# GDN's head norm moved into its back part, tokens on partitions

## The chip, the cores and the metric

One core of one Trainium2 chip. The metric is the device time of one execution in microseconds; the kernel before took 2085.72 us, the median of three runs (2085.12 to 2091.74).

## The reference, cut to what matters

The kernel computes three layers' worth of blocks in float32 for 528 tokens (16 meta tokens and 512) of width 1024. The change touches the first one, a gated delta net with 16 value heads of width 128, and in it the step between the recurrence and the output product:

```
o = chunk_gated_delta_rule(q, k, v, g, beta)
o = rms_norm(o, w_norm) * jax.nn.silu(z.reshape(b, t, GDN_V_HEADS, GDN_HEAD_DIM))
return o.reshape(b, t, GDN_V_DIM) @ w_out

def rms_norm(x, w):          # over the 128 features of one head and token
    return x * rsqrt(mean(x * x, axis=-1) + 1e-6) * w
```

## The kernel before, in words

The kernel is a row of stages, each a block with one program per engine; a stage ends when all engines have ended. Weights come in units of 128x2048 floats into one of four slots of `raw`; ScalarE casts a unit into a high part `whi` (`split_hi`, L153), VectorE makes the low part `wlo` (`split_lo`, L158), and every product of weights is three passes of TensorE over these (`product`).

The gated delta net has four stages. `gdn_front` makes q, k, v, z and the gates; v and z are spilled to DRAM. `gdn_back` (L1574) runs the recurrence. `head_norm` (L845) normalizes the heads, and `gated_down` (L2008) multiplies them with SiLU(z) and with the output weights.

`gdn_back` works on 20 units: 5 chunks (one of the 16 meta tokens, four of 128 tokens) by 4 groups of 4 heads. The software pipeline runs slots t = -1 to 22; `step(t, ...)` of each engine says which part of which unit it does in slot t, and in which order. That order is written out by hand, and each engine goes through it in order, with waits on semaphores. In slot t TensorE prepares unit t+1 (`prepare`: key-query products, transposed keys and values), multiplies the state for unit t (`old_values`), solves for unit t-1 (`new_values`), and makes the state's update and the output of unit t-2 (`update`, `output`). ScalarE copies the output of unit t-3 out of PSUM (`outputs`, L1829), exponentiates decays (`decays`, `weights`), copies the new values (`news`, L1824) and scales the values (`values`, L1816). VectorE multiplies by the decays (`attention` L1873, `differ` L1879), subtracts (`residual` L1890), makes the decayed copy of the new values (`decayed` L1898) and advances the state (`states` L1910). GpSimd adds the mask and multiplies q (L1658, L1664).

Slots 0 to 15 carry beside this the two last levels of the inversion of the 64 triangular matrices (`turn5` L1737 to `close6` L1764 on TensorE, `copy5`, `copy6` on ScalarE, `corner5` L1917, `corner6` on VectorE). TensorE's `open6` (L1756) waits for VectorE's `corner5`. In slots 0 to 7 VectorE also eliminates inside the 32x32 blocks of the second half (`second_half`, L1386 and L1389).

The output product (L1728, L1729) has the state and the new values as the stationary operand, so its result has features on partitions and tokens in rows: `ob`, one bank of PSUM, is the only one for it. ScalarE copies it to `qkv`, where q was (`out`). `yt` and the `raw` slots are the same memory; SP loads the first three units of the output weights there as the chunks are done with it (`ahead`).

`head_norm` goes over the 16 heads: GpSimd squares 128x528, TensorE sums over partitions with a matrix of ones, ScalarE takes Ln and Exp, VectorE multiplies by gain and root in place. The engines work on different heads at the same time.

`gated_down` splits units 0 and 1 first. Its SP program loads the fourth weight unit and then 16 tiles of z of 264 KB, three at a time. ScalarE takes their SiLU, VectorE the product with the heads, and both split it into high and low; TensorE uses each of the 16 tiles for units 0 and 1 as it comes, then runs units 2 to 7.

Of the kernel before, what the change touches and what calls it, by code (L numbers as in the profile page):

```python
# [23 lines left out]
P = 128  # L24
# [124 lines left out]
def split_hi(k, act, u, slot, used):  # L149

    act.wait_ge(k.raw_landed[slot], landed_value(u, slot))
    if used is not None:
        act.wait_ge(k.tile_full, used)  # L153
    k.nc.scalar.copy(k.whi[:, slot % SPLIT_SLOTS, :], k.raw[:, slot, :]).then_inc(k.hi_done, 1)  # L154


def split_lo(k, eng, u, slot):

    eng.wait_ge(k.hi_done, u + 1)
    s = slot % SPLIT_SLOTS  # L160
    eng.tensor_tensor(k.wlo[:, s, :], k.raw[:, slot, :], k.whi[:, s, :].bitcast(F32),  # L161
                      ALU.subtract).then_inc(k.lo_done, 1)
# [37 lines left out]
def unit_tiles(k, pe, u, slot, kts, xhi, xlo, first_slot, tile_free, x_ready=None):  # L200
# [4 lines left out]
    whi = k.whi[:, s, :].rearrange("p (k n) -> p k n", k=kts)  # L205
    wlo = k.wlo[:, s, :].rearrange("p (k n) -> p k n", k=kts)
# [559 lines left out]
def weight_ring(k, name, ctx):  # L766
    sb = lambda nm, shape, dt: ctx.enter_context(k.nc.sbuf_tensor(f"{name}_{nm}", shape, dt))
    k.whi, k.wlo = sb("whi", [P, SPLIT_SLOTS, UNIT], F32R), sb("wlo", [P, SPLIT_SLOTS, UNIT], F32R)
# [74 lines left out]


def head_norm(k, name, n, tile, ones, scale, gain, gain_src=None, then=(), gain_parts=()):  # L845

    nc = k.nc
    with ExitStack() as ctx:  # L850
        sb = lambda nm, shape: ctx.enter_context(nc.sbuf_tensor(f"{name}_{nm}", shape, F32))
        sq, rinv = sb("sq", [P, 4, T]), sb("rinv", [P, 4, T])
        g = sb("g", [P, n])
        sem = lambda nm: k.sem(f"{name}_{nm}")
        gain_in, squared, summed, log, inv, done = (sem(x) for x in (
            "gain_in", "squared", "summed", "log", "inv", "done"))
        gain_set = sem("gain_set")
        past4 = lambda j: not (isinstance(j, int) and j < 4)
        block = ctx.enter_context(stage(k))

        @block.sync
        def _(sp):
            if gain_src is not None:
                with nc.allow_non_contiguous_dma(reason="gains, feature on partitions"):
                    sp.dma_start(g[:, 0:gain_src.shape[1]], gain_src).then_inc(gain_in, 16)
            if then:
                load_ahead(k, sp, k.unit, then)

        @block.gpsimd
        def _(pool):  # L870
            def square(j, b):
                if past4(j):
                    pool.wait_ge(summed, j - 3)
                pool.tensor_tensor(sq[:, b, k.now], tile(j)[:, k.now], tile(j)[:, k.now], ALU.mult).then_inc(squared, 1)
            for cols, value in gain_parts:
                pool.memset(g[:, cols], value).then_inc(gain_set, 1)
            rounds(pool, n, square, 4)

        @block.tensor
        def _(pe):  # L880
            def one(j, b):
                pe.wait_ge(squared, j + 1)
                if past4(j):
                    pe.wait_ge(log, j - 3)
                for hf, half in enumerate(k.halves):
                    mm = pe.matmul(k.ps[b][:, hf, 0:k.width], ones, sq[:, b, half], start=True, stop=True)
                mm.then_inc(summed, 1)
            rounds(pe, n, one, 4)

        @block.scalar  # L890
        def _(act):
            def logarithm(j, b):
                act.wait_ge(summed, j + 1)
                if past4(j):
                    act.wait_ge(done, j - 3)
                nc.scalar.activation(parted(k, rinv[:, b, k.now]), filled(k, k.ps[b]), ACT.Ln, scale=scale,
                                     bias=k.eps[:, :])\
                    .then_inc(log, 1)
            def one(j, b):
                if not (isinstance(j, int) and j == n - 1):  # L900
                    logarithm(j + 1, (b + 1) % 4)
                act.wait_ge(log, j + 1)
                nc.scalar.activation(rinv[:, b, k.now], rinv[:, b, k.now], ACT.Exp, scale=-0.5).then_inc(inv, 1)
            nc.scalar.preload_act_table_set("natural_log_exp_and_others")
            logarithm(0, 0)
            rounds(act, n, one, 4)

        @block.vector
        def _(dve):
            if gain_src is not None:  # L910
                dve.wait_ge(gain_in, 16)
            if gain_parts:
                dve.wait_ge(gain_set, len(gain_parts))
            def one(j, b):
                dve.wait_ge(inv, j + 1)
                dve.scalar_tensor_tensor(out=tile(j)[:, k.now], in0=tile(j)[:, k.now], scalar=gain(g, j),
                                         in1=rinv[:, b, k.now], op0=ALU.mult, op1=ALU.mult).then_inc(done, 1)
            rounds(dve, n, one, 4)
# [655 lines left out]
def gdn_back(k, g, qkv, an, d, tmp, yt, yt0, out_unit):  # L1574
# [13 lines left out]
    with ExitStack() as ctx:  # L1588
# [32 lines left out]
        def _(sp):  # L1621
# [45 lines left out]
        def _(pe):  # L1667
# [50 lines left out]
            def output(u):  # L1718
# [11 lines left out]
                mm.then_inc(s.o_ready, 1)  # L1730
            def turn5(u):
# [35 lines left out]
            def step(t, real, level):  # L1767
# [22 lines left out]
        def _(act):  # L1790
            out = qkv[:, 0:2 * GQ, :].rearrange("p (o q) t -> p o q t", o=2)
# [33 lines left out]
            def outputs(u):  # L1825
                c, i = units[u]
                n, t = size(c), first_token(c)
                act.wait_ge(s.o_ready, u + 1)
                nc.scalar.copy(out[:, :, 2 * i:2 * i + 2, t:t + n],  # L1829
                               ob[:, :, 0:n].rearrange("p (q o) n -> p o q n", o=2)).then_inc(s.o_done, 1)  # L1830
# [12 lines left out]
            def step(t, real, level):  # L1843
# [1916 lines left out]
```

## Time and profile before

| what | value |
|---|---|
| median of three runs | 2085.72 us |
| the profiled execution: its time, its span | 2096.65 us, 2094.9 us |
| granted TensorE clock, mean | 0.951 |
| busy: TensorE, VectorE, ScalarE, GpSimd | 93%, 52%, 41%, 9% |
| back part of GDN, first and last instruction | 354 to 567.5 us |
| head norm | 567.8 to 593.4 us |
| output stage, first cast and first product | 593.7, 603.5 us |

The profile comes from one execution, slower than the median; differences are made within it. Granted clock 1.00 is 2.4 GHz and 0.50 is 1.2 GHz. "Idle before" names who released an engine that stood still. The slots of the back part can be told by ScalarE's copy of an output (L1829) at the start of each from t = 3 on:

| slot t | L1829 starts at, us |
|---|---|
| 3, 4, 5 | 389.47, 405.31, 420.80 |
| 6, 7, 8, 9 | 432.09, 443.29, 454.51, 464.65 |
| 10 to 15 | 474.05, 483.43, 492.82, 502.20, 511.58, 520.97 |
| 16 to 19 | 530.35, 537.36, 543.96, 550.55 |
| 20, 21, 22 | 557.72, 562.01, 566.30 |

### The profile page before, as it was taken

How to read it: one execution, taken by the hardware profiler on the slowest of the kernel's cores; microseconds unless marked ns; L12 is line 12 of the kernel's file. 1: busy time of each engine (PE TensorE's matmuls, PEld its weight loads, DVE VectorE, ACT ScalarE, POOL GpSimd, SP SyncE). 2: the span in 40 equal slices, each digit the busy share in tenths (PEclk: the TensorE clock that was granted, in tenths of full speed). 3: DMA queues.
4: the chain of work that ended last, by engine and by line, in shares of the span. 5: the costliest groups of instructions: out<-in, count | busy, mean ns of one | idle time of the engine just before them, and what ended most of it. 6: DMA issues, size and time to landing. Idle time of an engine off the chain costs nothing. (4 is left out here: it accounts for less than half of the span.)

```text
span 2094.9 us, 31713 instructions
## 1 busy us (share of the span) xinstructions
PE 1953.2 (93%) x12868; PEld 1744.9 (83%) x12868; DVE 1087.9 (52%) x1779; ACT 851.6 (41%) x1364; POOL 181.4 (9%) x198
## 2 busy tenths in 40 slices
PE   7999998999869999999999987899999998899988
PEld 6999998889769999999999965678888885787666
DVE  6657667675583344343453366544444447852243
ACT  6557742345472332333333144443332333424342
POOL 0001221022320000000000031000000002000101
PEclk9999998589989999999999999999999999999999
DMA  7223451113254223222222222223223322311101
GB/s 179 88 72 122 120 161 47 31 47 75 68 142 103 77 85 96 86 92 88 90 73 81 84 59 64 81 80 101 89 93 100 99 82 62 121 54 48 41 1 40
DMA packets 205246, 173.91 MB, mean 83 GB/s; under 512 B 41232, under 2 KB 180496, under 8 KB 205128
## 3 DMA queue, kind: packets, MB, share of 16 engines
q1 hardware_dynamic: 205128, 172.25, 27.7%
q8 instruction: 84, 1.38, 0.3%
q14 instruction: 34, 0.28, 0.0%
HBM read 161.40 MB, written 10.83 MB: 82 GB/s over the span
## 5 line engine op out<-in xcount | busy, mean ns | idle before, releaser
L161 DVE TENSOR_TENSOR main_wlo<-raw,main_whi 128x2048 fp32r<-128x2048 f32 x106 | 242.8, 2291 | 312.0 <-ACT main_whi L154 312.0
L154 ACT CAST main_whi<-raw 128x2048 fp32r<-128x2048 f32 x106 | 201.6, 1904 | 475.4 <-PE ps L176 474.1
L176 PE MATMUL ps<-ffn_xhi,main_whi 128*128 128x264 f32 (+1 forms) x768 | 206.5, 323 | 6.6 <-DVE ffn_xlo L646 6.6
L176 PE MATMUL ps<-ffn_xhi,main_wlo 128*128 128x264 f32 (+1 forms) x768 | 206.7, 324 | 0.0
L176 PE MATMUL ps<-ffn_xlo,main_whi 128*128 128x264 f32 (+1 forms) x768 | 206.6, 323 | 0.0
L176 PE MATMUL ps<-ffn_ahi,main_wlo 128*128 128x264 f32 (+1 forms) x768 | 205.2, 322 | 0.0
L176 PE MATMUL ps<-ffn_alo,main_whi 128*128 128x264 f32 (+1 forms) x768 | 205.0, 321 | 0.0
L176 PE MATMUL ps<-ffn_ahi,main_whi 128*128 128x264 f32 (+1 forms) x768 | 203.8, 320 | 0.0
L176 PE MATMUL ps<-gdn_xhi,gdnf_whi 128*128 128x264 f32 x768 | 162.2, 293 | 4.9 <-DVE gdn_xlo L517 4.4
L176 PE MATMUL ps<-gdn_xlo,gdnf_whi 128*128 128x264 f32 x768 | 158.0, 287 | 0.0
L176 PE MATMUL ps<-gdn_xhi,gdnf_wlo 128*128 128x264 f32 x768 | 157.9, 287 | 0.0
L176 PEld LDWEIGHTS ps<-ffn_xhi,main_whi 128*128 128x128 f32 x768 | 129.2, 190 | 19.2 <-issue 7.5
L176 PEld LDWEIGHTS ps<-ffn_xhi,main_wlo 128*128 128x128 f32 x768 | 128.9, 190 | 11.2
L176 PEld LDWEIGHTS ps<-ffn_xlo,main_whi 128*128 128x128 f32 x768 | 128.4, 190 | 11.6 <-issue 0.2
L176 PEld LDWEIGHTS ps<-ffn_ahi,main_whi 128*128 128x128 f32 x768 | 128.0, 188 | 11.6
L176 PEld LDWEIGHTS ps<-ffn_ahi,main_wlo 128*128 128x128 f32 x768 | 127.7, 188 | 10.8
L176 PEld LDWEIGHTS ps<-ffn_alo,main_whi 128*128 128x128 f32 x768 | 126.9, 188 | 11.3
L176 PEld LDWEIGHTS ps<-gdn_xhi,gdnf_whi 128*128 128x128 f32 x768 | 122.3, 191 | 6.6 <-issue 4.8
L359 DVE TENSOR_TENSOR h<-h,ps 128x528 f32<-128x528 f32 (+1 forms) x128 | 85.6, 691 | 80.2 <-PE ps L176 80.1
L176 PEld LDWEIGHTS ps<-gdn_xlo,gdnf_whi 128*128 128x128 f32 x768 | 120.8, 191 | 0.0
L176 PEld LDWEIGHTS ps<-gdn_xhi,gdnf_wlo 128*128 128x128 f32 x768 | 120.5, 191 | 0.0
L1158 DVE SCALAR_TENSOR_TENSOR gdnf_y<-gdnf_pre,gdnf_convw,gdnf_y 128x528 f32<-128x528 f32 x96 | 82.5, 861 | 61.7 <-ACT gdnf_y L1131 59.3
(474 smaller groups left out, 3878.1 us busy)
## 6 DMA issues: line engine op xcount, KB each, us to landing
raw<-in_ff_up_dram SPq DMA_DIRECT2D x32, 1024.0 KB, 5.4
raw<-in_ff_down_dram SPq DMA_DIRECT2D x32, 1024.0 KB, 5.1
raw<-in_gdn_in_dram SPq DMA_DIRECT2D x24, 1024.0 KB, 5.6
raw<-in_w_in_dram SPq DMA_DIRECT2D x14, 1024.0 KB, 5.3
raw<-in_mlstm_in_dram SPq DMA_DIRECT2D x12, 1024.0 KB, 5.3
raw<-in_gdn_out_dram SPq DMA_DIRECT2D x8, 1024.0 KB, 7.2
gdn_v_spilled<-gdnf_o SPq DMA_DIRECT2D x16, 264.0 KB, 2.2
gdn_z_spilled<-gdnf_o SPq DMA_DIRECT2D x16, 264.0 KB, 2.2
```

The lines of the kernel that those rows point to most:

```text
L154: k.nc.scalar.copy(k.whi[:, slot % SPLIT_SLOTS, :], k.raw[:, slot, :]).then_inc(k.hi_done, 1)
L161: eng.tensor_tensor(k.wlo[:, s, :], k.raw[:, slot, :], k.whi[:, s, :].bitcast(F32), ALU.subtract).then_inc(k.lo_done, 1)
L176: mm = pe.matmul(ps[:, b, 0:k.width], w, x[:, half], start=first and n == 0, stop=last and n == 2)
L359: dve.tensor_tensor(parted(k, acc[:, j, k.now]), parted(k, acc[:, j, k.now]), filled(k, k.ps[j % 4]), ALU.add).then_inc(s.down_free, 1)
L1158: dve.scalar_tensor_tensor(out=self.y[:, b, :], in0=self.pre[:, b, i:i + T], scalar=self.w[:, i, j:j + 1], in1=self.y[:, b, :], op0=ALU.mu ...
```

## The change

The head-norm stage is gone; the norm is done unit by unit in `gdn_back`. The operands of the output product are swapped, so that `ob` has tokens on partitions. In the next slot ScalarE squares it into `hs`, VectorE sums over the 128 features, ScalarE takes Ln and Exp of 4 numbers per token and scales the four heads into `hs`, TensorE transposes them back into `ob`, and VectorE copies `ob` to `qkv` with the gain per partition. The next output product waits for that copy instead of ScalarE's. Two loads of activation tables are placed at the head and the end of ScalarE's program.

The weight parts `whi`, `wlo` become one tensor per slot, and slot 0 lives through all stages, so that unit 0 of the output weights is split in slot 20 of the back part. In `gated_down` unit 1 alone is split at the start, and SP loads the first three z tiles ahead of the fourth weight unit.

```diff
 # gdn_back, SP: behind the first rows and values
+                sp.dma_start(gain[:, :], gain_col).then_inc(s.gain_in, 16)
 # TensorE
-                    pe.wait_ge(s.o_done, u)
+                    pe.wait_ge(s.h_done, u)
                 for h in range(GRP):
                     if c > 0:
-                        pe.matmul(ob[:, h, 0:n], st[:, GRP * i + h, :], eq[:, i, h, 0:n], start=True, stop=False)
-                    mm = pe.matmul(ob[:, h, 0:n], new[0:n, u % 2, h, :], dt[0:n, i, h, 0:n], start=c == 0, stop=True)
+                        pe.matmul(ob[0:n, h, :], eq[:, i, h, 0:n], st[:, GRP * i + h, :], start=True, stop=False)
+                    mm = pe.matmul(ob[0:n, h, :], dt[0:n, i, h, 0:n], new[0:n, u % 2, h, :], start=c == 0, stop=True)
+            def back(u):
+                pe.wait_ge(s.scaled, GRP * (u + 1))
+                for h in range(GRP):
+                    mm = pe.transpose(ob[:, h, 0:n], hs[0:n, h, :], k.ident[0:n, 0:n])
+                mm.then_inc(s.h_turned, 1)
 # TensorE's step: between prepare and open6
                     prepare(t + 1)
+                if real(t - 3):
+                    back(t - 3)
                 if level:
                     open6(t)
 # ScalarE
+            nc.scalar.preload_act_table_set("natural_log_exp_and_others")
-            def outputs(u):
+            def square(u):
                 act.wait_ge(s.o_ready, u + 1)
+                    act.wait_ge(s.h_turned, u)
+                nc.scalar.square(hs[0:n, :, :], ob[0:n, :, :]).then_inc(s.squared, 1)
+            def root(u):
+                act.wait_ge(s.summed, u + 1)
+                nc.scalar.activation(var[0:n, b, :], var[0:n, b, :], ACT.Ln, scale=1.0 / CH, bias=k.eps[0:n, :])\
+                    .then_inc(s.log, 1)
+                act.wait_ge(s.log, u + 1)
+                nc.scalar.activation(var[0:n, b, :], var[0:n, b, :], ACT.Exp, scale=-0.5).then_inc(s.inv, 1)
+            def scale(u):
+                act.wait_ge(s.inv, u + 1)
+                for h in range(GRP):
+                    nc.scalar.activation(hs[0:n, h, :], ob[0:n, h, :], ACT.Copy, scale=var[0:n, u % 2, h:h + 1])\
+                        .then_inc(s.scaled, 1)
 # ScalarE's step
                 if real(t - 3):
-                    outputs(t - 3)
+                    square(t - 3)
                 if level:
                     copy5(t)
+                if real(t - 3):
+                    root(t - 3)
+                    scale(t - 3)
                 if real(t - 1):
                     news(t - 1)
...
+                if t == nun:
+                    split_hi(k, act, u_out, 0, None)
             slots(step)
+            nc.scalar.preload_act_table_set("silu_and_others")
 # VectorE
+            def summed(u):
+                dve.wait_ge(s.squared, u + 1)
+                dve.reduce_sum(var[0:n, u % 2, :].unsqueeze(2), hs[0:n, :, :], AX.X).then_inc(s.summed, 1)
+            def leave(u):
+                dve.wait_ge(s.h_turned, u + 1)
+                dve.tensor_scalar(out[:, :, 2 * i:2 * i + 2, t:t + n], ob[:, :, 0:n].rearrange("p (q o) n -> p o q n", o=2),
+                                  gain[:, 0:1], None, ALU.mult).then_inc(s.h_done, 1)
 # VectorE's step
                     attention(t)
                 if real(t - 3):
+                    summed(t - 3)
                     states(t - 3)
...
                     corner5(t)
+                if real(t - 3):
+                    leave(t - 3)
                 second_half(t)
                 if t >= 0 and real(t + 1):
                     differ(t + 1)
+                if t == nun:
+                    split_lo(k, dve, u_out, 0)
 # gdn_out: no head_norm before gated_down
-    head_norm(k, "gdn_on", GV, tile, k.ones[:, :], 1.0 / P, lambda g, j: g[:, 0:1],
-              ins["gdn_norm"].rearrange("o p -> p o"))
-    k.loaded = NCH - 1
+    k.loaded, k.split = NCH - 1, 1
 # gated_down, SP
-            for u in range(loaded, RAW_SLOTS):
-                load_unit(k, sp, u0 + u, cols(u), ring(u))
             for kt in range(kts):
                 if kt >= 3:
                     sp.wait_ge(scaled, kt - 2)
                 sp.dma_start(z[:, kt % 3, :], gate_d.ap()[kt]).then_inc(z_in[kt % 3], 16)
+                if kt == 2:
+                    for u in range(loaded, RAW_SLOTS):
+                        load_unit(k, sp, u0 + u, cols(u), ring(u))
 # gated_down, ScalarE and VectorE
-            split_hi(k, act, u0, ring(0), t0)
-            split_hi(k, act, u0 + 1, ring(1), t0)
+            for u in range(split, 2):
+                split_hi(k, act, u0 + u, ring(u), t0)
```

## Rows read from the trace of the kernel before

**Rows 1.** The page, first line: busy us of each engine, share, instructions.
```profile
PE 1953.2 (93%) x12868; PEld 1744.9 (83%) x12868; DVE 1087.9 (52%) x1779; ACT 851.6 (41%) x1364; POOL 181.4 (9%) x198
```

**Rows 2.** Windows: stretch, length, busy time and instructions per engine, clock, DMA.
```profile
core 0: us, PE busy (x) PEld busy (x) DVE busy (x) ACT busy (x) POOL busy (x), PEclk, DMA share, GB/s
440.00:460.00 20.00, 16.37 (x160) 14.95 (x159) 16.28 (x34) 9.75 (x25) 5.10 (x5) 1.00 0.20 53
500.00:520.00 20.00, 19.80 (x194) 18.63 (x193) 10.22 (x30) 11.84 (x29) 5.84 (x6) 1.00 0.22 54
567.50:593.50 26.00, 18.57 (x64) 12.38 (x64) 19.83 (x16) 20.39 (x33) 21.08 (x16) 0.93 0.00 0
```

**Rows 3.** Timeline of slot 13: start, duration, engine, line, operation, count, idle before.
```profile
503.33 0.69 DVE L1873 TENSOR_TENSOR gdns_dt<-gdns_dt,ps 128x512 f32<-128x512 f32 x1
503.94 1.11 DVE L1910 SCALAR_TENSOR_TENSOR gdns_st<-gdns_st,gdns_el,ps 128x128 f32<-128x128 f32 x4
504.84 0.37 ACT L1837 COPY gdns_z<-ps 96x256 f32<-96x256 f32 x1 [1.10 <-PE ps L1744]
505.79 0.59 ACT L1824 COPY gdns_new<-ps 128x512 f32<-128x512 f32 x1 [0.58 <-PE ps L1706]
506.96 0.60 PE L1684 MATMUL ps<-ident,gdns_vf 128*128 128x128 f32 x4
507.60 1.14 ACT L1816 ACTIVATE gdns_vt<-ps,gdn_beta 128x128 f32<-128x128 f32 x4
507.66 0.41 PE L1756 MATMUL ps<-ident,raw 64*64 64x64 f32 x4
...
509.19 0.21 ACT L1796 ACTIVATE gdns_el<-gdns_eq 128x4 f32<-128x4 f32 x1
509.43 0.63 ACT L1798 ACTIVATE gdns_eq<-gdns_eq 128x512 f32<-128x512 f32 x1
```

**Rows 4.** Timeline of slots 20 to 22 and the start of the head norm.
```profile
560.03 0.39 PE L1728 MATMUL ps<-gdns_eq,gdns_st 128*128 128x128 f32 x2
...
562.01 0.59 ACT L1829 COPY wide<-ps 128x512 f32<-128x512 f32 x1 [2.81 <-PE ps L1729]
...
566.30 0.59 ACT L1829 COPY wide<-ps 128x512 f32<-128x512 f32 x1 [3.71 <-PE ps L1729]
567.78 1.28 ACT L904 ACT_TABLE_LOAD   x1 [0.89 <-PEq L95]
```

**Rows 5.** Timeline of the output stage's start, and its DMA issues (KB, us to landing).
```profile
593.72 3.70 ACT L154 CAST main_whi<-raw 128x2048 fp32r<-128x2048 f32 x2 [1.30 <-PEq L95]
595.65 4.49 DVE L161 TENSOR_TENSOR main_wlo<-raw,main_whi 128x2048 fp32r<-128x2048 f32 x2 [2.28 <-ACT main_whi L154]
600.53 1.32 ACT L2055 ACTIVATE gdn_out_z<-gdn_out_z 128x528 f32<-128x528 f32 x2 [1.81 <-DMA gdn_out_z<-gdn_z_spilled]
603.46 0.78 PE L176 MATMUL ps<-gdn_out_ahi,main_whi 128*128 128x264 f32 x2 [13.37 <-DVE gdn_out_alo L2074]
...
gdn_out_z<-gdn_z_spilled SPq DMA_DIRECT2D x16, 264.0 KB, 2.8
```

**Rows 6.** Line 2451, the only reduction: duration ns min/median/max, first and last start.
```profile
L2451 DVE TENSOR_REDUCE ml_var<-ml_sq x16: 406/408/419, 1222.0 to 1311.6; 128x2 f32<-128x256 f32 x16
```

**Rows 7.** Timeline of slot 4: VectorE's elimination and TensorE's `open6`.
```profile
411.96 0.41 DVE L1386 TENSOR_TENSOR gdn_tmp<-gdn_d 128x240 f32<-128x240 f32 x1
...
413.46 0.41 PE L1756 MATMUL ps<-ident,raw 64*64 64x64 f32 x4
```

**Rows 8.** Timeline of slots 17 and 18: VectorE's first and last instruction.
```profile
537.49 0.56 DVE L1868 COPY gdns_kd<-gdns_dt 128x4 f32<-128x4 f32 x1 [2.05 <-ACT gdns_dt L1803]
...
541.35 0.68 DVE L1879 TENSOR_TENSOR gdns_dt<-gdns_eq,gdn_tok 128x512 f32<-128x512 f32 x1
...
544.08 0.57 DVE L1868 COPY gdns_kd<-gdns_dt 128x4 f32<-128x4 f32 x1 [2.05 <-ACT gdns_dt L1803]
```

**Rows 9.** Timeline of slot 8's output product at half clock, and ScalarE's copy behind it.
```profile
461.09 0.54 PE L1728 MATMUL ps<-gdns_eq,gdns_st 128*128 128x128 f32 x2
...
464.65 0.59 ACT L1829 COPY wide<-ps 128x512 f32<-128x512 f32 x1 [2.58 <-PE ps L1729]
```

More of the change, by code:

```diff
@@ L153, in split_hi @@
         act.wait_ge(k.tile_full, used)
-    k.nc.scalar.copy(k.whi[:, slot % SPLIT_SLOTS, :], k.raw[:, slot, :]).then_inc(k.hi_done, 1)
+    k.nc.scalar.copy(k.whi[slot % SPLIT_SLOTS][:, :], k.raw[:, slot, :]).then_inc(k.hi_done, 1)
 def split_lo(k, eng, u, slot):
@@ L160, in split_lo @@
     s = slot % SPLIT_SLOTS
-    eng.tensor_tensor(k.wlo[:, s, :], k.raw[:, slot, :], k.whi[:, s, :].bitcast(F32),
+    eng.tensor_tensor(k.wlo[s][:, :], k.raw[:, slot, :], k.whi[s][:, :].bitcast(F32),
                       ALU.subtract).then_inc(k.lo_done, 1)
@@ L763, in split_rings, with weight_slot @@
     k.xhi, k.xlo = sb("xhi", [P, KD, T], F32R), sb("xlo", [P, KD, T], F32R)
-def weight_ring(k, name, ctx):
-    sb = lambda nm, shape, dt: ctx.enter_context(k.nc.sbuf_tensor(f"{name}_{nm}", shape, dt))
-    k.whi, k.wlo = sb("whi", [P, SPLIT_SLOTS, UNIT], F32R), sb("wlo", [P, SPLIT_SLOTS, UNIT], F32R)
+def weight_slot(k, name, ctx, slot):
+    sb = lambda nm, shape, dt: ctx.enter_context(k.nc.sbuf_tensor(f"{name}_{nm}{slot}", shape, dt))
+    k.whi[slot], k.wlo[slot] = sb("whi", [P, UNIT], F32R), sb("wlo", [P, UNIT], F32R)
 class ConvSilu:
@@ L842, in dve_end @@
         pass
[L845 to L918, printed above, removed]
@@ L1597, in gdn_back @@
         x5, z5, xz6 = sb("x5", [P, GRP, CH]), sb("z5", [P, GRP * 64]), sb("xz6", [P, 2, GRP * 64])
+        hs, var, gain = sb("hs", [P, GRP, CH]), sb("var", [P, 2, GRP]), sb("gain", [P, 1])
         v_in = [k.sem(f"gdns_v{j}") for j in range(VFS)]
@@ L1639, in _ @@
                     values(u)
+            with nc.allow_non_contiguous_dma(reason="128 gains, feature on partitions"):
+                sp.dma_start(gain[:, :], gain_col).then_inc(s.gain_in, 16)
             for t in range(nun):
@@ L1824, in news @@
                 nc.scalar.copy(new[0:n, u % 2, :, :], nb[0:n, :, :]).then_inc(s.new_done, 1)
-            def outputs(u):
-                c, i = units[u]
-                n, t = size(c), first_token(c)
+            def square(u):
+                n = size(units[u][0])
                 act.wait_ge(s.o_ready, u + 1)
-                nc.scalar.copy(out[:, :, 2 * i:2 * i + 2, t:t + n],
-                               ob[:, :, 0:n].rearrange("p (q o) n -> p o q n", o=2)).then_inc(s.o_done, 1)
+                if u >= 1:
+                    act.wait_ge(s.h_turned, u)
+                nc.scalar.square(hs[0:n, :, :], ob[0:n, :, :]).then_inc(s.squared, 1)
+            def root(u):
+                n, b = size(units[u][0]), u % 2
+                act.wait_ge(s.summed, u + 1)
[4 more added lines that the diff above has]
+            def scale(u):
+                n = size(units[u][0])
+                act.wait_ge(s.inv, u + 1)
+                for h in range(GRP):
+                    nc.scalar.activation(hs[0:n, h, :], ob[0:n, h, :], ACT.Copy, scale=var[0:n, u % 2, h:h + 1])\
+                        .then_inc(s.scaled, 1)
             def copy5(u):
@@ L1989, in gdn @@
             split_rings(k, "gdn", c2)
-            weight_ring(k, "gdnf", c2)
+            weight_slot(k, "gdnf", c2, 1)
             tiles = FrontTiles(qk, k.v_d, k.z_d, conv)
@@ L2016, in gated_down @@
     n, kts = KD, GV
-    u0, t0, loaded = k.unit, k.tile, k.loaded
+    u0, t0, loaded, split = k.unit, k.tile, k.loaded, k.split
     with ExitStack() as ctx:
@@ L2069, in _ @@
         def _(dve):
-            split_lo(k, dve, u0, ring(0))
-            split_lo(k, dve, u0 + 1, ring(1))
+            for u in range(split, 2):
+                split_lo(k, dve, u0 + u, ring(u))
             def low(kt):
```

44 lines of the change are left out of this document (26 added, 18 removed).

## The prediction

> **What bounds the kernel now.** Four views, from the wide one to the narrow one. The page's first line: TensorE 93% busy, ScalarE 41%, VectorE 52% [rows 1]. That is an average, and the change touches one stretch, from 354 to 603 us. The windows of that stretch come next [rows 2]: in 20 us of the back part's steady slots TensorE is busy for 19.80 and ScalarE and VectorE for half; in the 26.0 us of the head-norm stage it does 64 small matmuls, and GpSimd, ScalarE and VectorE share the work. Then the timeline of one steady slot [rows 3] and of the last slots [rows 4], to see who waits for whom. The chain that ended last lies in the kernel's final stage and says nothing here.
>
> I call a slot by the output product that ScalarE copies at its start; t counts as in the code. Slots 3 to 7 are paced by VectorE, which still eliminates there, 8 to 15 by TensorE, 16 to 18 by the loop VectorE, GpSimd, ScalarE, VectorE.
>
> **What goes.** The head-norm stage. ScalarE begins it at 567.78 [rows 4] and the next stage at 593.72 [rows 5]; both starts lie behind a like stage boundary, so 593.72 - 567.78 = **25.9 us** go.
>
> **What comes earlier in the output stage.** Before, its first product starts 603.46 - 593.72 = 9.7 us in, since the first gate tile stands behind a 1 MB weight load (SiLU at 600.53) [rows 5]. After, the gate tile is issued first; a 264 KB tile takes 2.8 us in the median [rows 5], say 2.3 when alone. ScalarE splits unit 1 alone (3.70/2 = 1.85), VectorE 2.25 behind it (4.49/2), until 4.1 to 4.2. Then the way from SiLU to product, 603.46 - 600.53 = 2.9, less the SiLU's 0.7 that ran beside the split: product at 6.3. Gain 9.7 - 6.3 = **3.5 us**. The bounds: if the 1 MB that now stands behind the third tile makes the fourth one late, all is lost (0); if the split did not count, 9.7 - 2.3 - 2.9 = 4.5. I take 3.5: the fourth tile lands about 8.5 in, and TensorE, at half clock there as before, wants it after 12. The split of unit 0 moves into slot 20, where ScalarE (1.85) and VectorE (2.25) do it beside an output product; it costs 0.1 in the next slot. Sum of gains: **29.4 us**.
>
> **What each slot gets.** In the slot after its product, a unit's path is now: square on ScalarE, sum on VectorE, Ln and Exp, four scalings, four transposes on TensorE, copy with gain on VectorE. Prices: square 0.59 in place of the copy's 0.59 [rows 4]; the sum is a reduction of 4x128, for which the trace has one of 2x128 at 0.41 [rows 6]; bounds 0.41 and 0.82, I take 0.68, near the 0.69 of the elementwise instruction of that size [rows 3]; the copy with gain likewise 0.68; back to back such a one advances VectorE by 503.94 - 503.33 = 0.61. Ln and Exp 0.21 each, each with a wait of the engine for itself: 509.43 - 509.19 = 0.24 a step. Four scalings 1.14 [rows 3], 1.03 until the next one starts. Four transposes 507.66 - 506.96 less the wait = 0.45. Swapping the operands of the output product costs nothing at 128x128; for the four short units it makes 128 columns of 16, in slots which TensorE doesn't pace (bound 0.6 in all). The new gain load on SP (bound 0.5) and ScalarE's table load at the head (1.28) lie beside the wait for the first rows; the table load for SiLU ends with the last copy. None is charged.
>
> Steady slot, by rows 3. ScalarE's queue: the z copy (504.84) ends 505.21; the sum is there (VectorE's attention starts 503.33, the sum follows 0.61 later, ends 504.6). So Ln 505.13, Exp 505.37, scalings from 505.61, and the copy of the new values, queued behind them, starts at 506.64 instead of 505.79: **0.86 late**. Behind it wait the decayed copy and the corner copy on VectorE, and for the corner copy waits TensorE's next transposes (507.66), late by the same 0.86. TensorE's four new transposes (0.45) fit into that gap. The later scalings of the values catch up, since ScalarE had idle time. So the slot grows by 0.86, not by TensorE's 0.45. Slots 9 to 15: 7 x 0.86 = 6.0; slot 8: 0.8.
>
> Slots 3 and 4: the copy with gain stands in VectorE's queue ahead of the elimination and waits for the transposes, and these stand behind TensorE's preparation, at half clock. In slot 4 that is until 413.46 + 0.9 for transposes and the way back, then 0.6 for preparation shifted and the copy itself: elimination at 414.9 instead of 411.96 [rows 7] = 3.0. Slot 3's own 2.6 of the same kind is taken up in slot 4 by VectorE's wait for the new values. Slots 5 to 7: sum 0.6, the new values 0.6 to 0.8 later than VectorE is ready, copy 0.15 to 0.6: 1.4 each, 4.2. **Slots 3 to 8: 3.0 + 4.2 + 0.8 = 8.0.**
>
> Slots 16 to 18 [rows 8]: VectorE's turn 541.35 - 537.49 = 3.86, then 544.08 - 541.35 = 2.73 through GpSimd and ScalarE. After: attention at 0.6, sum until 1.9, Ln, Exp, scalings until 3.4, new values until 4.0, decayed copy 4.04, copy with gain 4.64, difference at 5.25: 1.39 more, **4.2 in three**. Slot 19: its state product waits behind the transposes, **1.6**.
>
> Slots 20 to 22 have nothing beside the path. From an output product's end: square until 0.64, sum 1.36, scalings 1.88 to 3.02, transposes until 3.5, copy until 4.4 (4.8 in slot 20, behind the last new values), and then the next product of 562.01 - 560.03 = 2.0: 6.85 and 6.45 against 566.30 - 562.01 = 4.3 [rows 4]. That is 2.6 and 2.2. After the last one the next stage began 567.78 - 566.30 = 1.5 behind the copy's start; now the copy with gain ends 4.3 behind the square's start, and 0.3 go by at the boundary (VectorE's last instruction ended at 567.5, where the third window of rows 2 begins): 3.1. **Together 7.9.**
>
> Sum of costs: 8.0 + 6.0 + 4.2 + 1.6 + 7.9 = **27.7 us**.
>
> **The clock.** In this trace TensorE's half level comes in spells in just such stretches. The output product took 464.65 - 461.09 = 3.56 us at 1.2 GHz and 1.98 at 2.4 [rows 4, 9]: 1.6 us more. The one of rows 9 followed slots in which TensorE had stood for over a microsecond at the corner wait. After the change it stands 0.7 in each steady slot, 1.7 in slots 16 to 18 and 4 of 6.8 us in the tail. Bounds: 0 (the first spell falls where VectorE paces anyway) and 14 (below). I take two more slow products, **3 us**. The Trainium skill, "TensorE: Matmul & The Clock Gate", section "HAM oscillation — how this bites in real kernels", says that a nest which makes the array wait between bursts drops it to 1.2 GHz again and again. By it the tail would be slow throughout; this trace agrees in part, since slots with waits ran at 2.4 as well.
>
> **Sum:** -29.4 + 27.7 + 3 = +1.3 us. The profiled execution took 2096.65 (span 2094.9), so 2098 by its own measure; it stands 10.9 above the median of 2085.72. On the median: **2087 us**.
>
> **Rivals.**
>
> *The even exchange (forecast), 0.45.* 2079.5 to 2092, a term or two off by half its size. For it: both sums come from rows link by link.
>
> *Faster, 0.26.* The path is shorter than its queue says: if in the steady slots only TensorE's transposes counted, less its present idle, 7 x 0.3 = 2 instead of 6; and if slots 3 to 7 hid VectorE's wait (half of 7.2) and the clock stayed up (3), the cost would be 27.7 - 4 - 3.6 = 20, and the time 2085.7 - 29.4 + 20 = 2076. Against it: the corner wait is already TensorE's wait now.
>
> *Slower, 0.27.* The clock takes what the waits give it. At half clock slots 16 to 18 hold 6.3 us of TensorE work, some 11 when doubled in its busy part, so TensorE would pace them: 11 - 8 = 3 each, 9; two tail products and their transposes 2.5 each, 5. Together 14 in place of my 3: 2098. It decides against me (above 2092) from about five slow products on. For it: spells begin where TensorE waits. Against: in the 20 us from 440 it waited for 3.6 and the granted clock stayed 1.00 [rows 2].
>
> *It isn't one table, 0.02.* If Square, Ln, Exp and the scaled copy did not share a table, two loads of 1.28 us [rows 4] in 20 slots would add 51: 2137. Against: the head norm ran 32 Ln and Exp with one load (33 instructions) [rows 2].
>
> **Range and chances.** From 2075 (a third of the faster case lies below) to 2098 (a third of the slower one above). A measurement of this kernel tells 0.3%, 6.3 us, from no change: faster 0.26, same 0.45, slower 0.29.
>
> **What would show it.** No head-norm rows; the first output product some 6.3 us behind that stage's start; steady slots of about 10.2 us instead of 9.4 and the corner wait of TensorE grown to 0.6; slots 16 to 18 at 8.0 instead of 6.6; tail slots of 6.5 to 6.9, the last copy 4.4 behind its product; the granted clock from 530 on near 0.9. I am wrong if the steady slots stay near 9.8 (faster), if granted clock between slot 16 and the end of the back part is below 0.8 (slower), or if ScalarE loads tables inside the slots.

## The result, and the profile after

The changed kernel takes 2093.24 us (median of 14 runs, 2088.79 to 2096.86), the one before 2086.57 beside it (14 runs, 2080.64 to 2091.74). The ratio is 1.0027, 95% interval 1.0017 to 1.0038: slower by 5.6 us (3.5 to 7.9 by the interval), inside the 0.3% that the prediction called no change, though the interval reaches beyond it. (The two medians stand 6.7 us apart; the text goes by the ratio.) The profiled execution has a span of 2088.0 us and a mean granted clock of 0.953; it happens to be shorter than the profiled one of before, so spans can't be compared, and differences are made within the stretch.

The page's first line, beside [rows 1], shows how little the amount of work changed: 16 matmul records and 12 us of ScalarE more, 22 us of GpSimd less.

```profile
PE 1941.1 (93%) x12884; PEld 1735.1 (83%) x12884; DVE 1094.1 (52%) x1803; ACT 863.4 (41%) x1452; POOL 159.7 (8%) x182
```

The windows that answer to [rows 2], the third one moved to the back part's last slots (slots 19 to 22 are called the tail below). The steady slots stay at full clock although TensorE now idles a little; the tail does not.

```profile
core 0: us, PE busy (x) PEld busy (x) DVE busy (x) ACT busy (x) POOL busy (x), PEclk, DMA share, GB/s
440.00:460.00 20.00, 17.08 (x163) 15.72 (x164) 16.24 (x26) 8.78 (x25) 4.29 (x4) 1.00 0.19 50
500.00:520.00 20.00, 18.83 (x185) 17.66 (x184) 12.70 (x34) 13.08 (x37) 4.48 (x4) 1.00 0.24 54
572.00:593.00 21.00, 15.19 (x92) 14.55 (x91) 9.27 (x17) 7.01 (x17) 0.00 (x0) 0.76 0.00 0
```

A steady slot, against [rows 3]. Follow ScalarE: the root at 504.91 (two steps), the scalings at 505.48, and only then, at 506.50, the new values (L1761), whose product (L1634) ended at 505.55. Behind them the last transposes of the inversion (`open6`, here L1691) wait 0.58 us.

```profile
503.74 0.68 DVE L1824 TENSOR_REDUCE gdns_var<-gdns_hs 128x4 f32<-128x512 f32 x1
...
504.44 1.11 PE L1634 MATMUL ps<-gdns_vt,raw 128*128 128x128 f32 x8
504.64 0.37 ACT L1787 COPY gdns_z<-ps 96x256 f32<-96x256 f32 x1 [1.10 <-PE ps L1679]
504.91 0.30 ACT L1771 ACTIVATE gdns_var<-gdns_var,eps 128x4 f32<-128x4 f32 x1
505.24 0.20 ACT L1774 ACTIVATE gdns_var<-gdns_var 128x4 f32<-128x4 f32 x1
...
505.48 1.14 ACT L1779 ACTIVATE gdns_hs<-ps,gdns_var 128x128 f32<-128x128 f32 x4
...
506.50 0.61 ACT L1761 COPY gdns_new<-ps 128x512 f32<-128x512 f32 x1
...
507.20 0.60 PE L1664 MATMUL ps<-ident,gdns_hs 128*128 128x128 f32 x4
...
508.36 0.75 DVE L1831 TENSOR_SCALAR wide<-ps,gdns_gain 128x512 f32<-128x512 f32 x1
...
508.38 0.41 PE L1691 MATMUL ps<-ident,raw 64*64 64x64 f32 x4 [0.58 <-DVE raw L1886]
```

The last two slots and what follows them, against [rows 4, 5]. In slot 21 (from 583.95) and slot 22 nothing runs beside the unit's own path. In slot 20 TensorE stood for 2.26 us and came back at the full level: transposes 0.66 us, a state update 1.06. In slot 21 it stands for 3.15 us, and then its transposes take 1.12 us, a state update 1.92 and each pair of output matmuls 0.63 (0.39 before the wait): the half level.

```profile
579.94 0.66 PE L1664 MATMUL ps<-ident,gdns_hs 128*128 128x128 f32 x4 [2.26 <-ACT gdns_hs L1779]
...
580.43 1.06 PE L1644 MATMUL ps<-gdns_dec,gdns_kt 128*128 128x128 f32 x8
...
583.53 0.39 PE L1657 MATMUL ps<-gdns_new,gdns_dt 128*128 128x128 f32 x2
583.95 0.60 ACT L1767 ACTIVATE gdns_hs<-ps 128x512 f32<-128x512 f32 x1 [1.79 <-PE ps L1657]
...
587.06 1.12 PE L1664 MATMUL ps<-ident,gdns_hs 128*128 128x128 f32 x4 [3.15 <-ACT gdns_hs L1779]
...
587.97 1.92 PE L1644 MATMUL ps<-gdns_dec,gdns_kt 128*128 128x128 f32 x8
588.22 0.75 DVE L1831 TENSOR_SCALAR wide<-ps,gdns_gain 128x512 f32<-128x512 f32 x1 [1.92 <-PE ps L1664]
...
589.68 0.63 PE L1656 MATMUL ps<-gdns_st,gdns_eq 128*128 128x128 f32 x2
...
593.13 0.60 ACT L1767 ACTIVATE gdns_hs<-ps 128x512 f32<-128x512 f32 x1 [6.12 <-PE ps L1657]
...
597.40 0.75 DVE L1831 TENSOR_SCALAR wide<-ps,gdns_gain 128x512 f32<-128x512 f32 x1 [1.92 <-PE ps L1664]
598.50 1.90 ACT L154 CAST main_whi<-raw 128x2048 fp32r<-128x2048 f32 x1 [1.01 <-PEq L95]
...
605.20 0.78 PE L176 MATMUL ps<-gdn_out_ahi,main_whi 128*128 128x264 f32 x2 [7.84 <-DVE gdn_out_alo L2046]
...
608.39 0.65 ACT L2027 ACTIVATE gdn_out_z<-gdn_out_z 128x528 f32<-128x528 f32 x1 [3.02 <-DMA gdn_out_z<-gdn_z_spilled]
```

### The profile page after: what moved, and what is told of

It is laid out like the page before. It is cut to its first block and busy times, and to the rows that moved or that the text cites. A ratio compares the mean times of both kernels' runs of the same rounds, so it can differ in the third digit from the quotient of the medians.

```text
span 2088.0 us, 31755 instructions
## 1 busy us (share of the span) xinstructions
PE 1941.1 (93%) x12884; PEld 1735.1 (83%) x12884; DVE 1094.1 (52%) x1803; ACT 863.4 (41%) x1452; POOL 159.7 (8%) x182
## 5 line engine op out<-in xcount | busy, mean ns | idle before, releaser
L161 DVE TENSOR_TENSOR main_wlo<-raw,main_whi 128x2048 fp32r<-128x2048 f32 x118 | 271.1, 2297 | 316.2 <-ACT main_whi L154 316.2
L154 ACT CAST main_whi<-raw 128x2048 fp32r<-128x2048 f32 x118 | 224.6, 1904 | 473.8 <-PE ps L176 472.7
L349 DVE TENSOR_TENSOR ffn_alo<-wide,ffn_ahi 128x528 fp32r<-128x528 f32 (+1 forms) x64 | 44.8, 701 | 87.8 <-ACT ffn_ahi L307 87.8
L176 PE MATMUL ps<-mls_xhi,main_whi 128*128 128x264 f32 (+1 forms) x320 | 80.8, 318 | 5.7 <-DVE mls_xlo L646 4.9
L442 ACT ACTIVATE wide<-wide 128x528 f32<-128x528 f32 (+1 forms) x64 | 40.9, 639 | 106.9 <-DVE wide L449 106.9
L176 PE MATMUL ps<-gdn_xhi,main_whi 128*128 128x264 f32 x384 | 81.0, 292 | 4.4 <-DVE gdn_xlo L517 4.4
L176 PE MATMUL ps<-gdn_xhi,gdnf_whi 128*128 128x264 f32 x384 | 81.6, 294 | 1.0 <-DVE gdnf_wlo L161 1.0
L176 PE MATMUL ps<-sec_xhi,main_whi 128*128 128x512 f32 x176 | 75.8, 430 | 5.6 <-DVE sec_xlo L517 4.4
```

The costliest lines, as they stand in the source:

```text
L154: k.nc.scalar.copy(k.whi[slot % SPLIT_SLOTS][:, :], k.raw[:, slot, :]).then_inc(k.hi_done, 1)
L161: eng.tensor_tensor(k.wlo[s][:, :], k.raw[:, slot, :], k.whi[s][:, :].bitcast(F32), ALU.subtract).then_inc(k.lo_done, 1)
L176: mm = pe.matmul(ps[:, b, 0:k.width], w, x[:, half], start=first and n == 0, stop=last and n == 2)
L349: dve.tensor_tensor(alo[:, par, m, k.now], k.a[:, m % 2, k.now], ahi[:, par, m, k.now].bitcast(F32), ALU.subtract).then_inc(s.lo, 1)
L442: k.nc.scalar.square(k.a[:, m % 2, k.now], k.b[:, m % 2, k.now]).then_inc(s.a_ready, 1)
```

## The sum, term by term

A slot is measured as in the slot table of before, from ScalarE's first instruction on a unit's output to the next one. All in us; the last column is a second profile of the changed kernel (e7 below).

| term | forecast | before → after | measured | again |
|---|---|---|---|---|
| head-norm stage | -25.9 | 25.94 → none | -25.9 | -25.9 |
| slots 3 to 8 | +8.0 | 75.18 → 81.75 | +6.6 | +6.7 |
| slots 9 to 15 | +6.0 | 65.70 → 72.15 | +6.5 | +6.4 |
| slots 16 to 18 | +4.2 | 20.20 → 24.79 | +4.6 | +4.6 |
| slot 19 | +1.6 | 7.17 → 8.81 | +1.6 | +1.9 |
| slot 20 | +2.6 | 4.29 → 7.12 | +2.8 | +2.8 |
| slot 21 | +2.2 | 4.29 → 9.18 | +4.9 | +5.1 |
| slot 22 to the next stage | +3.1 | 1.48 → 5.37 | +3.9 | +3.8 |
| first product of the output stage | -3.5 | 9.74 → 6.70 | -3.0 | -3.2 |
| from it to the first accumulation into `h` | 0 | 24.92 → 25.86 | +0.9 | +1.3 |
| clock, spread over the slots | +3 | in the rows above | | |
| sum | +1.3 | 238.91 → 241.73 | +2.8 | +3.4 |

## Experiments

Each ran beside the kernel before on the same chip, but not all on one chip, so it is the ratio that compares them; a value by the ratio is good to about 3 us either way, a difference of two to about 4. "By the ratio" below is (ratio - 1) x 2087 us. "Stretch" is the time from slot 3 to the first accumulation, in one profile.

| kernel | median | ratio, 95% | by the ratio | stretch |
|---|---|---|---|---|
| before | | 1 | 0 | 238.9 |
| changed | 2093.24 | 1.0027 (1.0017 to 1.0038) | +5.6 | 241.7 |
| changed, again (e7) | 2093.31 | 1.0026 (1.0010 to 1.0042) | +5.4 | 242.4 |
| e1 layout only | 2086.64 | 0.9990 (0.9974 to 1.0007) | -2.1 | 233.7 |
| e2 all but the norm | 2088.11 | 0.9996 (0.9982 to 1.0011) | -0.8 | 237.0 |
| e11 = e2, split earlier | 2087.17 | 0.9991 (0.9976 to 1.0006) | -1.9 | 235.1 |
| e3 new values first | 2087.35 | 1.0001 (0.9987 to 1.0014) | +0.2 | 239.2 |
| e4 busy TensorE | 2090.27 | 1.0013 (0.9997 to 1.0028) | +2.7 | 236.6 |
| e12 = e4, split earlier | 2091.80 | 1.0013 (0.9998 to 1.0029) | +2.7 | 237.8 |
| e5 second bank | 2091.38 | 1.0021 (1.0005 to 1.0038) | +4.4 | 237.2 |
| e9 = e5, split earlier | 2086.46 | 0.9997 (0.9985 to 1.0010) | -0.6 | 235.7 |
| e6 orders together | 2086.60 | 0.9993 (0.9978 to 1.0009) | -1.5 | 234.9 |
| e8 = e6, split earlier | 2082.25 | 0.9973 (0.9960 to 0.9986) | -5.6 | 231.1 |
| e10 = e8, busy TensorE | 2077.60 | 0.9954 (0.9936 to 0.9971) | -9.6 | 227.3 |

**The parts without the norm.** e1 is the kernel before with one tensor of split weights per slot, slot 0 living throughout; e2 adds the split of unit 0 in slot 20 and the gate tiles ahead of the fourth weight unit.

> The kernel before, with one thing of the change: the weight parts are one tensor per slot, and slot 0 lives through all stages; the head norm stays. Theory A (the change acts only in the delta net's part, and its cost and gain lie there): no difference, ratio 1.000 within its interval, 2086.6 us. Rival B (the tensors' new places cost the stages that stream weights some microseconds, which would make up for the difference between the 2.7 us that the two profiles show up to the second stage and the 5.6 us of the medians): 2089 to 2090 us.

> As e1, and the output stage as in the change (unit 0 of the output weights split in slot 20, the first three gate tiles ahead of the fourth weight unit); the head norm stays a stage of its own. Theory A: the first product comes 3 us earlier in its stage and 0.9 of it is given back when the fourth gate tile is late behind the 1 MB of weights: 2.1 to 2.5 us faster, 2084.3 us. Rival B: all is given back, because the gate tiles pace the sixteen steps anyway: 2086.6 us.

The layout shows no cost (-2.1, interval -5.4 to +1.5). e2 took 2088.11 us where 2084.3 were expected. Its output stage starts its first product 6.39 us in, as reckoned (6.3), but the time does not tell its 3 us: -0.8 with an interval of 3 us to either side. Its slot 21 went from 4.29 to 5.44 us behind the split. The norm itself, change against e2, costs 6.4 us by the ratio and 4.8 in the stretch.

**The queue on ScalarE (e3).** The new values ahead of root and scalings, the transposes behind `open6`, from slot 8 on:

```diff
+                if t >= 8 and real(t - 1):
+                    news(t - 1)
                 if real(t - 3):
                     root(t - 3)
                     scale(t - 3)
```

> The changed kernel with another order from slot 8 on: ScalarE copies the new values ahead of Ln, Exp and the scalings, TensorE's transposes of the heads stand behind open6, VectorE's copy with gain behind the difference. Theory A (in slots 8 to 15 the slot grows by the delay of the new values in ScalarE's queue, 0.92 us, and not by TensorE's 0.45 us of transposes; in 16 to 18 by VectorE's two instructions and the late new values): slots 8 to 15 fall from 10.31 to about 9.83 us, 16 to 18 from 8.13 to about 7.3, in all 6 us, 2087 us. Rival B (TensorE's added work and waits for the scalings set the slot, wherever they stand): 10.3 us and 2093 us, as the changed kernel.

The time came as expected, but by luck, since what was to bring it, the steady slot, did not come: 10.24 us, not 9.83 (10.31 in the change). The stretch of its one profile gives 2.6 us, the ratio 5.4. The steady slot in this kernel:

```profile
505.49 0.59 ACT L1763 COPY gdns_new<-ps 128x512 f32<-128x512 f32 x1 [0.58 <-PE ps L1634]
...
506.30 0.68 DVE L1871 TENSOR_TENSOR gdns_dec<-ps,gdns_kd 128x512 f32<-128x512 f32 x1
...
507.55 0.41 PE L1691 MATMUL ps<-ident,raw 64*64 64x64 f32 x4 [0.28 <-DVE raw L1890]
...
508.49 0.66 PE L1664 MATMUL ps<-ident,gdns_hs 128*128 128x128 f32 x4
...
508.99 1.06 PE L1644 MATMUL ps<-gdns_dec,gdns_kt 128*128 128x128 f32 x8
509.19 0.75 DVE L1835 TENSOR_SCALAR wide<-ps,gdns_gain 128x512 f32<-128x512 f32 x1 [0.97 <-PE ps L1664]
...
510.09 0.46 PE L1656 MATMUL ps<-gdns_st,gdns_eq 128*128 128x128 f32 x2
```

This slot starts at 501.90, the one of the change at 502.00. Counted from there, the new values are copied 0.91 us earlier, and `open6` starts 0.73 earlier, since VectorE's sum holds the decayed copy for 0.2. The rest puts it back: the transposes (0.5, in the change hidden in TensorE's wait) now stand on TensorE's path, and the output product starts at 510.09, 0.15 behind the end of the copy with gain. (In slot 20 of the change it also starts 0.15 behind that copy, and there the profile names it as what the product waited for.) So a second path was within 0.07 us of the first. What e3 gained came in the steady slots (0.5), in slots 17 and 18 (0.6) and in the tail (slot 21 at 7.90).

**The clock (e4).** Matmuls of 128 columns into a bank nothing reads, ahead of the transposes' wait, 3 in slots 16 to 18, 8 in 19 and 20, 12 in 21 and 22:

```diff
+                for _ in range({16: 3, 17: 3, 18: 3, 19: 8, 20: 8, 21: 12, 22: 12}.get(t, 0)):
+                    pe.matmul(flat[6][:, 0:P], k.ident[:, :], k.ident[:, :], start=True, stop=True)
                 if real(t - 3):
                     back(t - 3)
```

> The changed kernel with matmuls of the identity by itself into a bank that nothing reads, 3 ahead of the transposes in slots 16 to 18, 8 in 19 and 20, 12 in 21 and 22, where TensorE stands and waits for the scalings. Theory A (the granted clock falls to half after such waits and costs about 3.3 us from slot 19 on: slot 21 took 9.18 us against 7.12 of slot 20): slot 21 at 7.1 us, granted clock 1.00 from 540 us to the end of the back part, 2090 us. Rival B (the half level comes at its own time): the same granted clock and 2093 us or more.

The granted clock from 572 to 593 is 1.00, where it was 0.76. Slot 21 fell to 6.76 us, slot 19 to 7.81, the end to 4.91. These are its transposes, update and output in slot 21, to be held against the rows of after above (a pair of records stands for one matmul here, so 12 show as x24):

```profile
581.18 2.84 PE L1716 MATMUL ps<-ident 128*128 128x128 f32 x24
...
584.49 0.66 PE L1664 MATMUL ps<-ident,gdns_hs 128*128 128x128 f32 x4 [0.47 <-ACT gdns_hs L1781]
...
584.99 1.06 PE L1644 MATMUL ps<-gdns_dec,gdns_kt 128*128 128x128 f32 x8
585.19 0.75 DVE L1833 TENSOR_SCALAR wide<-ps,gdns_gain 128x512 f32<-128x512 f32 x1 [1.46 <-PE ps L1664]
```

The mechanism is shown by the rows: 1.92 → 1.06 and 1.12 → 0.66. In slots 19 to 22 the profile gives 3.9 us back (25.11 → 21.70, 5.37 → 4.91). The ratio gives 2.9, which by itself its interval would not tell from nothing.

**The single bank (e5) and all orders (e6).** e5 takes a second bank for the output and a second `hs` from unit 15 on, and puts the transposes behind the output product from slot 19 on. e6 adds e3's order in every slot, VectorE's copy with gain inside the elimination's steps in slots 3 to 7, and the late transposes from slot 17 on. e7 is the changed kernel once more beside them.

```diff
+        obank = lambda u: xb5 if u >= 15 and u % 2 else ob
 # output
-                    pe.wait_ge(s.h_done, u)
+                    pe.wait_ge(s.h_done, u if u < 15 else u - 1)
```

> The changed kernel with two output banks in the tail: units 15, 17 and 19 write their output product into the bank that the inversion left free after slot 15, the scaled heads have two buffers, and from slot 19 on TensorE makes the transposes behind the output product and VectorE advances the state ahead of the sum. Theory A (in the tail each output product waits for the whole path square, sum, root, scalings, transposes, copy of the one before, since there is one bank): slots 19 to 21 fall from 8.8, 7.1 and 9.2 us to about 5.5 each, 2085 us. Rival B (one path through the engines is needed in any order, and what is taken away in front comes back behind, or the slot waits for the state): slots 20 and 21 stay above 6.5 us, 2091 us or more.

> As e5 (the tail's order from slot 17 on), and in every slot ScalarE copies the new values ahead of the root, the transposes stand behind open6, and VectorE's copy with gain stands in the middle of the elimination (slots 3 to 7) or behind the difference. After e3 a steady slot is expected at 10.2, not 9.8 us (the sum on VectorE, the four transposes and the wait of the output product for the copy add up to 0.86 by themselves). Theory A (in slots 3 to 7 VectorE paces, and its wait for the transposes and the late new values cost about 0.8 of the 1.4 us of a slot): slots 5 to 7 at about 12.4 instead of 12.7 us, slot 3 at 16, slots 16 to 18 at 7.3, in all 2080 us, below the kernel before. Rival B (only the tail gives): 2084 us, as e5.

> The changed kernel once more, on the same chip as e5 and e6, for the comparison and for a second profile of it. Theory A (costs by slot as in its first profile; TensorE's spells at half clock fall differently each time and move the back part by up to 5 us, as they did between the profiles of the kernel before and of e1): steady slots 10.31, slots 17 and 18 at 8.13, 1.002 to 1.004 of the kernel before, 2093 us. Rival B (the first profile's slow slots 19 and 21 are always there): 8.8 and 9.2 us again.

e7 repeats the steady slots (10.31) and the ratio, and its slots 19 and 21 take 9.02 and 9.38 us: the slow tail is there again, as its rival said, while the spells in slots 4 and 8 moved (14.46 and 11.02 in the first profile, 16.25 and 9.44 here).

e5 and e6 both missed their numbers, by 6 to 7 us; e5 gained 1.0 against e7 by the ratio, less than can be told, and e6 6.9. Slot 19 came as expected (5.54), 20 and 21 did not (6.70 and 8.04 in e5, 6.21 and 9.17 in e6). The end of e5's slot 20, and its slot 21:

```profile
579.56 1.94 ACT L154 CAST main_whi<-raw 128x2048 fp32r<-128x2048 f32 x1
...
581.36 0.64 ACT L1772 ACTIVATE gdns_hs<-ps 128x512 f32<-128x512 f32 x1
581.53 2.29 DVE L161 TENSOR_TENSOR main_wlo<-raw,main_whi 128x2048 fp32r<-128x2048 f32 x1 [0.36 <-ACT main_whi L154]
583.73 1.12 DVE L1884 SCALAR_TENSOR_TENSOR gdns_st<-gdns_st,gdns_el,ps 128x128 f32<-128x128 f32 x4
...
585.00 2.05 PE L1646 MATMUL ps<-gdns_dec,gdns_kt 128*128 128x128 f32 x8 [4.62 <-DVE gdns_st L1884]
```

The split that lay hidden beside a slow slot now stands in the path: the cast ahead of the square, the difference ahead of the state. TensorE waits 4.62 us and comes back at the half level.

**The split moved (e8, e9), and TensorE kept busy as well (e10).** `split_hi` in slot 14 and `split_lo` in 15; e10 adds to e8 6, 8 and 8 matmuls in slots 20 to 22.

```diff
-                if t == nun:
+                if t == 14:
                     split_hi(k, act, u_out, 0, None)
```

> The kernel with all the orders together (e6_all), and in addition the output product's first weight unit is split into its two halves in slots 14 (ScalarE's cast, 1.91 us) and 15 (VectorE's difference, 2.29 us) instead of slot 20. In e5_banks the shortened tail was held up there: ScalarE's cast of 1.94 us stood ahead of slot 21's square, VectorE's difference of 2.29 us ahead of its state update, and TensorE idled for 4.6 us. Theory A: the split is what ate the shortening. Then slots 20 and 21 fall from 6.2 and 9.2 us to about 5.5 each, slots 14 and 15 grow by 1 to 2 us each at most (ScalarE and VectorE both have some idle time in a steady slot), and the time falls from 2086.6 to about 2083, with 2081 to 2085 as range. Rival B: the slots are long because of the TensorE clock, which falls once the engine has idled: slot 21 stays over 7.5 us and the time at 2086 to 2087.

> The changed kernel with the second output bank and the second buffer from unit 15 on (e5_banks), and in addition the split of the first weight unit moved from slot 20 to slots 14 and 15. Theory A (the split is what ate the shortening): slot 21 falls from 8.0 to about 5.5 us, slot 20 from 6.7 to about 5.5, slots 14 and 15 grow by 0 to 2 us together, and the time falls from 2091.4 to about 2088.5 (2087 to 2089.5). Rival B (the clock): slot 21 stays at 7 us or more and the time stays at 2091.

> The kernel of e8_split_all with 6, 8 and 8 matmuls of 128 columns more in slots 20, 21 and 22, into a bank that nothing reads there, ahead of the transposes' wait, so that TensorE does not idle long. If TensorE's clock falls in the tail of e8_split_all and costs there and in the table load's stage and the first product behind it, this takes 1 to 3 us off its time, to about 2081. If with a slot of 5.5 us the clock does not fall any more, the time is that of e8_split_all within 0.5 us, or up to 1 us more.

e9 against e5: -5.0 by the ratio, -1.5 in the stretch. Slots 20 and 21 are 5.32 and 6.94 (6.70 and 8.04 in e5), slots 9 to 15 grew by 1.3 for it. e8 against e6: -4.1 by the ratio, -3.7 in the stretch, slots 20 and 21 at 5.31 and 6.84. The times came as expected or better (2082.25 in the range of 2081 to 2085, 2086.46 for 2087 to 2089.5). But the split explains slot 20, and slot 21 only in part: about 5.5 were expected there. The rest of slot 21 is the clock, as the rival of both had it. In e8 TensorE stands for 1.97 us, does the update at the full level, and falls to the half level in the output product:

```profile
578.62 1.13 PE L1646 MATMUL ps<-gdns_dec,gdns_kt 128*128 128x128 f32 x8 [1.97 <-DVE gdns_st L1884]
...
579.86 0.64 PE L1660 MATMUL ps<-gdns_new,gdns_dt 128*128 128x128 f32 x2
```

e10 against e8, on one chip: 2082.25 → 2077.60, more than the 1 to 3 us expected. The stretch is 3.8 us shorter, but 1.8 of it lies in slots 3 to 8, where the two kernels are the same. What the matmuls give where they stand, in slots 20 to 22, is 2.1 us: slot 21 6.84 → 5.32, slot 22 to the next stage 5.94 → 5.37. Its tail, at a granted clock of 1.00 from 563 to 585:

```profile
574.19 0.60 ACT L1774 ACTIVATE gdns_hs<-ps 128x512 f32<-128x512 f32 x1 [0.80 <-PE ps L1660]
...
574.43 1.95 PE L1719 MATMUL ps<-ident 128*128 128x128 f32 x16
...
575.30 1.11 DVE L1886 SCALAR_TENSOR_TENSOR gdns_st<-gdns_st,gdns_el,ps 128x128 f32<-128x128 f32 x4
...
576.55 1.13 PE L1646 MATMUL ps<-gdns_dec,gdns_kt 128*128 128x128 f32 x8 [0.18 <-DVE gdns_st L1886]
...
579.51 0.60 ACT L1774 ACTIVATE gdns_hs<-ps 128x512 f32<-128x512 f32 x1 [0.76 <-PE ps L1660]
```

579.51 - 574.19 = 5.32 us for slot 21. This version is faster than the kernel before, if by less than half a percent: 0.9954, interval 0.9936 to 0.9971, from six runs.

**Controls (e11, e12).**

> A control: the head norm as before the change (e2_outstage), with what helped the changed kernel beside it: two allocations of the split weights, the first unit split ahead, the gate tiles loaded ahead, and here the split in slots 14 and 15 instead of slot 20. It tells whether the 2077.6 us of e10_split_all_busy come from the changed norm or from these neighbours. If from the norm: this one stays at 2086 to 2088, as e2_outstage did (2088.11), slot 21 going from 5.44 back to 4.29 us. If from the neighbours: 2082 or less.

> The changed kernel with the additional matmuls of e4_busy (2090.27) and the split moved to slots 14 and 15, and no reordering at all. Its tail's slots are 7.8, 7.1 and 6.8 us, and in slots that long ScalarE's cast and VectorE's difference have room: if the split costs only where the tail has been shortened, the time stays at 2090 within 1 us. If it costs in any tail, it falls to about 2087.

e11 stays at 0.9991, so e10's gain is not that of the neighbours without the changed norm. (It was not tried with extra matmuls; in its slots 20 and 21 TensorE is busy for 6.67 of 8.60 us at clock 1.00, so there is little idle to fill.) e12 took 2091.80, where 2089 to 2091 were expected; it has e4's ratio, 1.0013, with 3 us of interval to either side; it is the rows that show that the split costs nothing in a tail that was not shortened. Slots 19 to 21 are what they were in e4 (21.69 and 21.70), while slots 14 and 15 are 0.7 and 0.6 us longer and slot 16 is 0.4 shorter.

## Why the prediction came out as it did

**The exchange was right, its time at the upper edge.** Steady slot (0.92 for 0.86), slots 16 to 19 and slot 20 stand within 0.5 us of their terms. TensorE's wait at the corner is 0.58, as forecast (0.6); one table load stands at either end and none between. The likeliest case was 2079.5 to 2092. The measured median of 2093.24 lies just above it, where the slower rival begins; by the ratio, 2085.72 x 1.0027 = 2091.4, it lies just inside. The sign that was named for the slower rival, a granted clock below 0.8 from slot 16 to the end of the back part, did not come: it is 0.89. So the terms bear out the even exchange, with +5.6 for +1.3 us.

**Mis-sized: slots 3 to 8, and the baseline.** 8.0 forecast, 6.6 measured, but against a row of before with its own spells of half clock (slots 4 and 8). Against e1, where slots 3 to 8 take 71.51, the change adds 10.2: 3.9 in slots 3 and 4 (3.0 forecast, all in slot 4; slot 3 alone grew by 2.4, which was said to be taken up), 3.9 in slots 5 to 7 (4.2), and 2.5 in slot 8, which takes 9.44 in e7 and would then be 0.9 (0.8). So the prices of the work were near, and it is luck that the sum of the profile came out as near as +2.8. The stretch of e1, e2 and e11 is 1.9 to 5.2 us shorter than in the profiled execution of before, while their times lie 0.8 to 2.1 below it. The baseline of the sum had about 2 us in it that a usual execution lacks (an estimate from these three). Against e1 stretch and time agree: 8.0 and 7.7 us.

**The clock: near in size, short in what it slows.** 3 us were taken for two slow output products; e4 gives back 3.9 in slots 19 to 22. Slot 21 alone took 2.7 more than its term, with output, update and transposes at the half level, and slot 22 took 0.8 more: the copy with gain ends 5.0 behind the square's start, not 4.3, and its transposes are at the half level too. At the full level, in e4, slots 20 and 21 take 7.13 and 6.76 us for 6.85 and 6.45: the path itself was priced within 0.3. The rival in which slots 16 to 18 become TensorE's did not come: they take 8.54, 8.13 and 8.12, and e4's extra matmuls there change nothing (8.55, 8.13, 8.14). The granted clock is 0.76 from 572 to 593 and 1.00 in the steady slots, which wait for 0.58 each. The Trainium skill ("TensorE: Matmul & The Clock Gate", section "HAM oscillation — how this bites in real kernels") tells of bursts that are shorter than the waits between them and start slow each time. This trace agrees in part: the tail is slow after its wait of 3.15 us and not after the one of 2.26, and the steady slots, whose waits are much shorter than their work, are not such a case.

**The output stage.** The fourth gate tile is late for ScalarE, which idles 3.02 us for it (SiLU at 608.39) behind the 1 MB weight load. But TensorE, at the half level there, needs what ScalarE does behind that wait (the split of the third tile) only at 610.46, 12.0 us into the stage, and waits 0.2 us; the fourth tile itself it needs after 12, as the prediction had it. From its first product to the first accumulation it is busy for 25.66 of 25.86 us. e12 and e11 wait as long for the tile (2.85 and 2.65) and need 25.12 and 25.21. So the 0.9 us by which this row grew is not the late tile's, and its cause stays open. The gain itself was added as 3.5, where 9.7 - 6.3 is 3.4; 3.0 came.

**Missed: the split beside a short slot.** It was charged 0.1 us in the next slot. In e2, with the slots of before, it cost 1.15 (slot 21 4.29 → 5.44). In the change itself the long slots hide it, as e12 shows.

**Missed: that the steady slot has two paths of one length.** ScalarE's queue was read rightly as what set the slot; that its removal would bring 0.07 us and not 0.5 was seen only in e3. "Which wait ends last" tells what adding work costs; what taking it away brings depends on the next path, which has to be priced too.

**Open.** By its terms the change adds 2.8 to 3.4 us in the stretch, by time 5.6 ± 2. The baseline accounts for about 2 of the rest; whether the stages behind bring anything can't be told from single profiles. How much e10's extra matmuls bring beyond the 2.1 us of the tail is open too.

## What to carry to other kernels

Moving a stage's work into a pipeline that has idle engines costs what it adds to the path of one slot, times the slots, and most in the tail, where nothing runs beside it. Twenty short chains over idle engines cost as much as a whole stage of 26 us. Give the longer path a second buffer and bank and put its steps in an order that lets the rest pass (here 6.9 us by the ratio, e6 against e7), keep large fillers out of the shortened slots (4.1), and keep TensorE at work across the wait (2.1 in the tail's rows): together that turned +5.6 us into -9.6.

An edit that is free beside a slow slot is to be priced again when the slot gets faster.

## What the runs showed of the hardware

- A sum over 128x512 into 128x4 on VectorE takes 0.68 us, the same as an elementwise instruction of that size (0.69); the copy with gain out of PSUM in another order takes 0.75.
- ScalarE's step on 128x4 with the bias takes 0.30 us and the next, waiting for it, starts 0.33 behind; the one without 0.24.
- Equal code (slots 3 to 8 of before and e1) took 75.18 and 71.51 us in two executions, the difference lying in slots 4 and 8. One profile of each kernel doesn't settle 5 us here.
- 22 matmuls that compute nothing shortened the slots they stand in by 2.1 us and kept the granted clock at 1.00 in the tail (0.88 without them, e8, 565 to 589). The medians differ by 4.7 us (2082.25 → 2077.60, ten and six runs).
- The length of one wait of TensorE did not tell the level behind it: 2.26 us in slot 20 of the change left it at full, 1.97 us in slot 21 of e8 was followed by the half level about 1 us into the work.
